# Gathers of second rows in turn with first rows, tiles of one head, three second rows of sixteen added on VectorE

## What is computed

```python
def block(xb):                       # xb: normed tokens
    q = (xb @ w_query).reshape(tb, PEER_HEADS, 2, PEER_KEY_DIM // 2)      # 8 heads
    s = jnp.einsum('thpd,pnd->thpn', q, sub_keys)                         # two times 128 scores
    top_s, top_i = lax.top_k(s, k)                                        # k = 16
    cand_s = top_s[:, :, 0, :, None] + top_s[:, :, 1, None, :]
    cand_i = top_i[:, :, 0, :, None] * PEER_N_KEYS + top_i[:, :, 1, None, :]
    best_s, best_j = lax.top_k(cand_s.reshape(tb, PEER_HEADS, k * k), k)
    idx = jnp.take_along_axis(cand_i.reshape(tb, PEER_HEADS, k * k), best_j, axis=-1)
    gate = jax.nn.softmax(best_s, axis=-1)
    u = expert_u[idx]                                                     # first rows
    act = jax.nn.gelu(jnp.einsum('thkd,td->thk', u, xb))
    return jnp.einsum('thk,thkd->td', gate * act, expert_v[idx])          # second rows
```

## Time and profile before

| stretch, us | what runs | TensorE busy | VectorE | GpSimd | DMA share | GB/s |
|---|---|---|---|---|---|---|
| 0 to 290 | attention of layer 0, first index list | 270.95 | 95.51 | 27.78 | 0.21 | 72 |
| 345 to 418 | tile 1 and 2, with output projection and queries | 66.53 | 52.90 | 47.11 | 1.03 | 405 |
| 418 to 763 | seven plain tiles | 223.97 | 214.78 | 213.26 | 0.91 | 341 |
| 763 to 1175 | eight tiles, first mixer pass | 370.64 | 272.24 | 249.06 | 0.99 | 378 |
| 1175 to 1584 | eight tiles, second mixer pass | 347.25 | 267.78 | 250.06 | 0.97 | 369 |
| 1584 to 1928 | seven plain tiles | 220.70 | 214.97 | 215.74 | 0.92 | 341 |
| 1928 to 1971 | last second rows, final norm | 30.11 | 3.89 | 8.07 | 0.43 | 158 |

### The profile page before, as it was taken

One profiled execution on the slowest core, in us unless ns is written; L12 is line 12 of the kernel. 1 busy time (PEld: TensorE's weight loads), 2 busy tenths in 40 slices (PEclk: granted clock), 3 DMA queues, 4 the chain that ended last, 5 costly groups with the idle time before them and its releaser, 6 DMA issues.

```text
span 1970.9 us, 17348 instructions
## 1 busy us (share of the span) xinstructions
PE 1577.1 (80%) x4322; PEld 776.4 (39%) x4322; DVE 1155.1 (59%) x2896; ACT 301.0 (15%) x950; POOL 1046.2 (53%) x1143
## 2 busy tenths in 40 slices
PE   8999979896666666999989968977999666666666
PEld 3467636352222222444434524433445322222222
DVE  2433236665666667666677666655676666666661
ACT  1033112121111111321111211200111111111111
POOL 1110026666666666566656656656565665666662
PEclk9955599997878788999989979988999988888887
DMA  5210118998999899999999999999999999999985
GB/s 175 87 44 11 74 69 323 403 351 332 346 337 340 335 349 336 347 389 397 395 370 375 405 379 359 377 404 350 361 360 400 360 355 337 338 346 335 342 334 191
DMA packets 184121, 616.73 MB, mean 313 GB/s; under 512 B 19275, under 2 KB 20811, under 8 KB 184054
## 3 DMA queue, kind: packets, MB, share of 16 engines
q0 software_dynamic: 152064, 553.72, 74.3%
q1 hardware_dynamic: 31990, 62.23, 8.6%
HBM read 614.83 MB, written 1.05 MB: 312 GB/s over the span
## 4 chain that ended last, share of the span: by engine, by line
PE 53%; issue 16%; POOL 10%; DVE 10%; DMA 8%; ACT 1%; POOLq 0%; DVEq 0%; SPq 0%; ACTq 0%
PE bank L816 23%; PE bank L616 12%; POOL arena L556 10%; DVE arena L1445 8%; DMA arena<-peer_u,idx_now 8%; PE bank L804 4%; PE bank L717 3%; PE bank L802 2%; PE bank L932 1%; PE bank L689 1%; PE bank L678 1%; DVE h L1472 1%; PE bank L780 1%; PE bank L605 1%; PE bank L766 1%
## 5 line engine op out<-in xcount | busy, mean ns | idle before, releaser
L816 PE MATMUL bank<-arena 128*128 128x512 f32 x2112 | 925.8, 598 | 21.0 <-ACT arena L1077 19.7
L1445 DVE CUSTOM_DVE_ANT_0 arena<-arena,bank 128x1024 f32<-128x1024 f32 x528 | 628.9, 1219 | 478.3 <-DMA arena<-peer_u,idx_now 468.8
L556 POOL DMA_INDIRECT arena<-peer_v,idx_now x528 | 511.2, 968 | 434.1 <-PE bank L816 331.6
L816 PEld LDWEIGHTS bank<-arena 128*128 128x128 f32 x2112 | 405.7, 193 | 548.0 <-issue 547.8
L556 POOL DMA_INDIRECT arena<-peer_u,idx_now x528 | 499.2, 945 | 196.8 <-issue 135.5
L802 PE MATMUL bank<-skT,q_now 128*128 128x256 f32 x66 | 34.0, 612 | 331.0 <-DVE dots L1445 274.9
L616 PE MATMUL bank<-wring,hT 128*128 128x512 f32 (+5 forms) x604 | 260.8, 589 | 2.5 <-ACT hT L973 1.6
L616 PEld LDWEIGHTS bank<-wring,hT 128*128 128x128 f32 (+1 forms) x604 | 108.5, 182 | 145.5 <-issue 139.8
L1077 ACT ACTIVATE arena<-con,wgt 128x128 f32<-128x128 f32 (+1 forms) x528 | 157.8, 387 | 31.6 <-DVEq L1468 31.6
L802 PEld LDWEIGHTS bank<-skT,q_now 128*128 128x128 f32 x66 | 14.4, 271 | 351.6 <-issue 351.6
L1071 ACT ACTIVATE gl<-gl 128x16 f32<-128x16 f32 x33 | 7.1, 215 | 786.2 <-DVEq L1460 786.2
(11 more groups left out here) (158 smaller groups left out, 1045.8 us busy)
## 6 DMA issues: line engine op xcount, KB each, us to landing
wring<-gla_w_in SPq DMA_DIRECT2D x12, 2048.0 KB, 19.8
arena<-peer_u,idx_now POOLq DMA_INDIRECT x528, 6.6
arena<-peer_v,idx_now POOLq DMA_INDIRECT x528, 6.8
wring<-gla_w_out SPq DMA_DIRECT2D x4, 2048.0 KB, 19.6
wring<-peer_w_query SPq DMA_DIRECT2D x4, 2048.0 KB, 23.0
wring<-attn_w_in SPq DMA_DIRECT2D x2, 2048.0 KB, 8.3
wring<-attn_w_out SPq DMA_DIRECT2D x2, 2048.0 KB, 7.8
gws<-peer_w_query SPq DMA_DIRECT2D x2, 2048.0 KB, 10.4
```

What stands on the lines that cost most here:

```text
L556: nc.gpsimd.indirect_dma_start(out=rows[:, k % RING, :], out_offset=None, in_=table.rearrange("l e d -> (l e) d"), in_offset=bass.Indirect ...
L816: last = nc.tensor.matmul(yacc[:, 512 * i:512 * i + 512], wplace[:, k, :], vrow[:, k % RING, 512 * i:512 * i + 512], start=(k == 0), stop= ...
L1445: v.tensor_tensor_reduce(out=urow[:, k % RING, :], in0=urow[:, k % RING, :], in1=xrep, scale=1.0, scalar=0.0, op0=ALU.mult, op1=ALU.add, a ...
```

## The change

- **Tiles.** A tile is one head of one block of 128 tokens (`GATHERED`), so a partition is a token. Tile 0 is still the meta tokens, 16 by 8. There are again 33 tiles with 16 + 16 gathers of 512 KB each. In layer 0 tiles 1 to 8 are the heads of block 1, 9 to 16 those of block 2; in layer 1 likewise.
- **Copies.** The token of a partition now lies in `hn` as it is. The masks, the repetition on TensorE and the copies of queries and of the index list go (the repetition stays for the meta tokens alone, once, into `hn`). The dots read `urow` and `hn`.
- **Order of gathers.** In round i GpSimd issues for each k the second row of tile i-1 and then the first row of tile i. The last round has second rows alone.
- **Second rows.** VectorE adds those with k = 4, 9 and 14 itself (`add_second`, one instruction over 1024 columns into `h`), in front of the dot of the same k. TensorE mixes the other 13, now with a diagonal matrix, and sums over all eight heads of a block in PSUM; the addition to `h` comes once for each block instead of once for each tile.
- **Weights.** One Gelu instruction on ScalarE takes the place of several small ones on VectorE around a tanh.
- **Rounds.** VectorE's choice for tile i+1 stands between dots 6 and 7 of tile i. The mixer's stages stand in fixed rounds (`STAGE_AT`) at one of two slots; stages 0 and 1 of a pass are in one round. All rounds are written out, there is no loop.

The core of the diff:

```diff
-TT = P // PH
+GATHERED = [(0, 0, 0)] + [(layer, b, x) for layer in range(2) for b in (1, 2) for x in range(PH)]
+TILES = len(GATHERED)
+SHARE = (4, 9, 14)
...
+        STAGE_AT = {(2 + 8 * full + n, slot): (t, full) for full in (1, 2)
+                    for t, (n, slot) in enumerate(((0, 0), (0, 1), (1, 1), (2, 1), (3, 1), (4, 1), (5, 0)))}
...
-                for kind, table, rows, used, landed in (("u", io["peer_u"], urow, u_used, u_in), ("v", io["peer_v"], vrow, v_used, v_in)):
-                    for k in range(TOPK):
...
+            def gather(kind, g, k):
+
+                layer = GATHERED[g][0]
+                if kind == 0:
+
+                    at_least(pool, u_used, TOPK * g + k - RING + 1)
+                elif k >= RING:
+                    wait_second_used(pool, g, k - RING)
+                elif g:
+                    wait_second_used(pool, g - 1, k + RING)
...
+                for k in range(TOPK):
+                    gather(1, i - 1, k)
+                    if i < TILES:
+                        gather(0, i, k)
...
-                    v.tensor_tensor_reduce(out=urow[:, k % RING, :], in0=urow[:, k % RING, :], in1=xrep, scale=1.0, scalar=0.0,
+                    if g and k in by_vector(g - 1):
+                        add_second(g - 1, k)
+                    dve.wait_ge(u_in[k % RING], landings(g, k))
+                    v.tensor_tensor_reduce(out=urow[:, k % RING, :], in0=urow[:, k % RING, :], in1=hn[:, b, :], scale=1.0, scalar=0.0,
...
+            def add_second(g, k):
+                b = GATHERED[g][1]
+                dve.wait_ge(v_in[k % RING], landings(g, k))
+                at_least(dve, v_added, ADDED[g] + by_vector(g).index(k))
+                v.scalar_tensor_tensor(out=h[:, b, :], in0=vrow[:, k % RING, :], scalar=wgt[:, g % 2, k:k + 1], in1=h[:, b, :],
+                                       op0=ALU.mult, op1=ALU.add).then_inc(v_added, 1)
...
-            for i in range(2):
-                add_to_h(("ao", 0, i), 0, i)
...
+                dot(i, range(0, 3))
+                if (i, 0) in STAGE_AT:
+                    gla(*STAGE_AT[i, 0])
+                if i == 26:
+                    norm(6, [1])
+                dot(i, range(3, 7))
+                if i + 1 < TILES:
+                    choose(i + 1)
+                dot(i, range(7, 11))
```

More of the change, by code:

```diff
@@ L578, in _ @@
-            gathers(25, 1, 1, lambda: root(small[:, 1:2], small[:, 4:5], 1))
-            gathers_pairs(26, 3, 1)
-            gathers(32, 0, 1)
+            def gather(kind, g, k):
[6 more added lines that the diff above has]
+                    wait_second_used(pool, g - 1, k + RING)
+                table, ring, landed = ((io["peer_u"], urow, u_in), (io["peer_v"], vrow, v_in))[kind]
+                nc.gpsimd.indirect_dma_start(
+                    out=ring[:, k % RING, :], out_offset=None, in_=table.rearrange("l e d -> (l e) d"),
+                    in_offset=bass.IndirectOffsetOnAxis(ap=idx[:, g % 3, k:k + 1], axis=0)).then_inc(landed[k % RING], 16)
@@ new lines, in chosen, with mixer_root @@
+            def chosen(g):
+                pool.wait_ge(idx_ready, g + 1)
+            def mixer_root(t, full):
+                b = PASSES[full][0]
+                if t == 0:
+                    root(small[:, b:full + 1], small[:, 3 + b:4 + full], full + 1 - b)
+                elif t == 5:
+                    root(gms[:, 0:4], gms[:, 4:8], 4)
+                elif t == 6:
+                    root(small[:, full:full + 1], small[:, 3 + full:4 + full], 1)
+            chosen(0)
+            for k in range(RING):
+                gather(0, 0, k)
@@ L821, in gla @@
+                    last.then_inc(v_mixed, 1)
             def gla(t, full):
@@ L934, in gla @@
                             end(last, un)
-            prepare(0, 0, 0)
+            for half in range(2):
+                wait_emptied(pe, ("tr_o", 0, half))
+            out_project(0, 0)
+            out_project(0, 1)
+            spread_gains(1)
+            for b in (1, 2):
+                tr_stream("tr_o", None, b)
+            meta_queries()
             for b in (1, 2):
@@ new lines, in choose @@
+                steps.settle()
+                for s in range(2):
+                    steps.did(v.match_replace(rest[:, s, :], top[:, s, 0:8], half[s], -3e38))
+                    steps.did(v.max_index(top_i[:, s, 0:8], top[:, s, 0:8], half[s]))
+                steps.settle()
+                dve.sem_inc(scores_taken, 1)
+                for s in range(2):
+                    steps.did(v.max(top[:, s, 8:16], rest[:, s, :]))
+                steps.settle()
+                for s in range(2):
+                    steps.did(v.max_index(top_i[:, s, 8:16], top[:, s, 8:16], rest[:, s, :]))
@@ L1476, in _ @@
-            FIRST, SECOND = range(0, TOPK // 2), range(TOPK // 2, TOPK)
-            def tile(g, b, layer, j, side=None):
-                pick(g + 1, j)
-                dot(g, SECOND)
-                weigh(g)
-                choose(g + 1, layer)
-                if side:
-                    side()
-                dot(g + 1, FIRST)
-                add_experts(g, b)
+                zs = z[:, g % 2, :]
+                steps.did(v.reciprocal(zs[:, 2:3], zs[:, 1:2]))
+                dve.wait_ge(u_used, TOPK * (g + 1))
```

503 lines of the change are left out of this document (233 added, 270 removed).

## The result

The changed kernel took 2008.49 us (median of four runs, 1997.46 to 2016.07), the kernel before 1966.41 us beside it (1961.98 to 1974.46): a ratio of 1.021, 95% interval 1.017 to 1.025. The profiled execution has a span of 2005.3 us. The page first: the span, the busy lines, the DMA share in slices, the largest groups of VectorE and GpSimd, and one that the kernel before has only at a few places.

The account below looks back on a forecast made before the run. No engine was full: GpSimd's 39.8 us of gathers plus 10 us of waits for TensorE's mixing made the 49.2 us tile. Forecast: 326.6 + 1616 + 30 + 46 = 2019 us of span, so 2017 us; range 1875 to 2095.

Parts of the forecast that it names:

- 12 rounds with mixer stages: Rounds holding mixer work: 50.5 us each like any round, plus 30 us together for TensorE's excess and the mixer's two-operand instructions.
- T = 53: T is the time of one round of 16 gather pairs; 53 us was the range's slow end, put at 2095 us.
- The price per gather: GpSimd gathers begun during VectorE instructions with two SBUF operands wait for their end: 39.8 + 10.9 = 50.7 us a round.
- the would-show list: Signs to check: gathers 1.2 to 1.3 us, gaps 0.30, dots 1.22, DMA share 0.85 to 0.9; wrong if rounds under 48 us.
- rows of dots: Dots worked off back to back after the choice of experts: one gather gets through in 2.28 us, costing 3.8 us a round.
- lone dots: The other 9 dots of a round, standing alone: each meets nearly one gather start and costs 0.6 us, together 5.4 us.
- the additions and the products of the choice: VectorE's additions ahead of single dots and two products in the choice of experts delay gathers by 1.7 us a round.
- rival 1: Gathers slip between the dots, which fall in step with gather starts: 46 to 48.7 us a round, 1923 at 47.5; chance 0.24.
- The contested moment: About 0.13 us after its start, a gather needs something that a VectorE instruction with two SBUF operands holds until its end.
- Rival 3: VectorE and GpSimd exclude each other wholly, on each gather and dot: 53.5 us a tile, 2115 us in all; chance 0.06.
- stages of 17 us fit into the ring's slack: Mixer stages on TensorE other than the round with two: the ring of 8 rows, 19.9 us, absorbs them without cost.
- Rival 2: The port costs nothing and DMA is the bound: 41.4 us a round at 405 GB/s, 1801 us in all; chance 0.08.

## Why the prediction was right, and where it was not

It said 2017 us and a slower kernel; 2008.5 us and slower it is. By its own terms:

| term | predicted | measured (span) |
|---|---|---|
| start, until tile 1's gathers | 326.6 | 319.7 |
| 20 plain rounds | 20 x 50.5 = 1010 | 952 |
| 12 rounds with mixer stages | 12 x 50.5 + 30 = 636 | 694 |
| the end | 46 | 39.6 |
| sum | 2019 | 2005 |

The two large errors, 58 us each, cancel. The forecast's time is as much luck as sense, and so is its direction: by its own account a faster plain round would have made a faster kernel, and it was the mixer that made it slower. The next points matter more than the sum. (One sum of it is slightly off: T = 53 gives a span of 2099 us, not 2095.)

**The price per gather: mechanism right, size too high.** Gathers of 1.15 us (foreseen 1.2 to 1.3), gaps of 0.30, dots still 1.22: as the would-show list has it. DMA share 0.97 at 360 GB/s is above its 0.85 to 0.9 at 330, and a plain round of 47.3 us is under the 48 at which the text calls itself wrong on this term. Split by what delayed each gather, seven plain rounds (424.9 to 753.8) give per round: 3.2 us in rows of dots (predicted 3.8), 2.9 us at lone dots (predicted 5.4), 0.8 us at the additions and the products of the choice (1.7). With the 39.8 us of free gathers that is 46.7 us, and the rounds are 47.0. The step that failed is "a dot of 1.22 us meets one start in nearly each case (starts are 1.245 us apart) and costs half its length": six gathers a round are delayed at lone dots, half a microsecond each, not nine at 0.6. The free phase that was said to be "hardly any" exists, because a gather begun up to 0.04 us after the dot is let through. In plain rounds rival 1 (T of 46 to 48.7) was the case.

**The contested moment.** The prediction put it 0.13 us after a gather's start, and at the dot's end the rows bear this out: of the 119 gathers that begin in the last 0.12 us of a dot, 114 keep 0.94 to 0.95 us (the other five meet the next long instruction), and the 264 that begin earlier and are delayed end 0.81 to 0.87 us after it. At the dot's start it had nothing: 0.04 us after the start a gather gets through (634.78), 0.05 us after it one waits (605.03). With 0.13 us that puts the dot's claim about 0.17 us after its own start, an estimate from these two.

**Rival 3 fell.** Dots beside gathers are 1.21 to 1.30 us; the most that one gives is 0.09 us. The Trainium skill, "SBUF — State Buffer", section "SBUF: two separate sides", has both sides wait for the whole instruction; these rows show one side only.

**The mixer: "stages of 17 us fit into the ring's slack" failed.** The slack was compared with the stage's own work, but TensorE first waits for VectorE's result, as long again (18.94 us), with unmixed rows behind it. The wait and the work count together against 19.9 us of ring. And three of the seven stages need a square root from GpSimd, which lies between gathers there; VectorE's norms wait 56.4 us for such roots in all, 12.1 us in the kernel before, and the step past GpSimd's queue was not costed. Of the 88 us by which the twelve rounds exceed 12 x 50.5, the two of 77.6 and 78.1 us hold 55; the prediction had its one long round where the two stages meet (68 us, measured 72.8) and none here. Moving the stage behind the thirteenth row halved the first wait and took 66 us off these rounds on chip 3 (40 us between chips 2 and 3).

**Rival 2 (the port costs nothing, 41.4 us) fell:** the port does cost. But its 41.4 us was too low in any case. The roof of 405 GB/s was read from a stretch with weight loads beside the gathers; the plain stretch of the earlier trace rows, 341 GB/s at a share of 0.91, points to 375 GB/s, and the changed kernel's 360 at 0.97 to 371, so 45 us for 16.8 MB (an estimate). With the token in PSUM and gathers at 1.00 us no round was under 44 us. On the chips where this ran, late updates held many rounds, and most of those with under 2 us of them still took 44 to 46 us at shares of 0.95 to 0.99. By that estimate a plain round of 47 us would come down by about 2 us without the port's delay; for the first chip no run shows it.

**Not foreseen: the chip.** The prediction's sign holds for the chip on which it was measured. On chips where the old order suffers from late updates, a plain tile of before is 54 us and the same change wins.

## What to carry to other kernels

- The price of a shared port depends on phase: where both sides take nearly equally long, look whether one side's starts are set by the other's, and don't average over random starts.
- A stage put into a ring of buffers costs its own work plus whatever its first instruction waits for; compare that sum with the ring, and look at each helper instruction on the queue that fills the ring.
- If a delay on one engine is taken away and the time stays, count the waits for an engine's own results: with the gathers shorter, VectorE's had grown from 126 to 222 us. And a gain or loss of 2 to 4% was reversed by another chip, so measure on more than one before the order of work is fixed.

## What the runs showed of the hardware that was not expected

- Chips differ by 10% for one and the same kernel (1966 us on the first, 2173 to 2202 us on four others), and by 4% for another. Each chip was used in one session, so what else differed between the first comparison and the later runs isn't told apart from the chip. In the traces VectorE's own semaphore updates are late by 0.5 to 5.4 us on the four, mostly with gathers near their free pace of 1.245 us. In the trace of the kernel before on chip 12 (last seven tiles edited) they sum to 73 us, but its span is 195 us above the first chip's; VectorE's waits for ScalarE's tanh, 123.8 us there, are part of the rest. With half rows and the token in PSUM over 100 late updates came after 6 us with a DMA share under 0.95, so a full DMA is not needed for them. What delays them no run shows.
- The exclusion is one-sided: a gather begun 0.05 us or later into a dot (0.10 us into an addition of a second row), and more than 0.12 us before its end, waits for that end; the dot gives at most 0.09 us.
- An instruction of 0.13 us on GpSimd between two gathers costs nothing; it lies in the 0.30 us between them.
- ScalarE loads a function table twice a round in the changed kernel, 63 loads of 1.28 us (one group of them above), since the two functions of the weights now alternate. That is 81 us, on an engine with 17% of work, and hidden except for the waits of VectorE's weights, 40.8 us in all against 6.3 us before.
